# Prompt attention: where PE forms the former step's values in steps of at most four tiles

## The chip, the cores and the metric

The kernel runs on one core of one Trainium2 chip. The metric is the device time of one execution in microseconds, as the median of three runs.

## The reference

One layer of a hybrid decoder. RMSNorm and an adaLN modulation, one input projection for all heads, then attention for half of the channels and a short convolution for the other half, both gated by SiLU, an output projection, a gated residual, a last RMSNorm. There is a prompt of 1024 tokens and a sample part of 8 times 4 new tokens with a cache of 2048. The change touches the prompt's attention alone. It has 16 heads of 64 in two groups, and three branches: compressed blocks of 64 keys, selected blocks, and a window of 512. With 1024 keys there are 16 blocks and 16 are selected, so that the selected branch is plain causal attention.

```python
lg = jnp.einsum('bqghd,bngd->bghqn', qs, k_cmp) + tab[t5_bucket(d_cmp)].transpose(2, 3, 0, 1)
p_cmp = masked_softmax(lg, m_cmp)
o_cmp = jnp.einsum('bghqn,bngd->bqghd', p_cmp.astype(v_cmp.dtype), v_cmp)
...
lg = jnp.einsum('bqghd,bgqnkd->bghqnk', qs, ks) + b_sel.transpose(0, 1, 5, 2, 3, 4)
...
lg = jnp.einsum('bqghd,bwgd->bghqw', qs, k_win) + tab[t5_bucket(d_win)].transpose(2, 3, 0, 1)
...
return g[:, :, 0] * o_cmp + g[:, :, 1] * o_sel + g[:, :, 2] * o_win
```

## The kernel before

Each engine has its program written out by hand, and engines meet by semaphores. The prompt's attention is done in 32 units: a unit `u` is four heads on one tile of 128 queries. The tile is `TILE_ORDER[u % 8]` = 0, 2, 4, 6, 7, 5, 3, 1, so there are four passes of eight units. A unit has two steps, `w = 2u` for the selected branch and `w = 2u + 1` for window and compressed branch: 64 steps, 16 a pass. `tiles_of(w)` is the number of key tiles of a step: in a pass 1, 2, 3, 4, 5, 6, 7, 6, 8, 6, 6, 6, 4, 5, 2, 3. The last tile of an odd step is the compressed branch's.

A step has four quarters `h = 0..3`. PE's loop (L1456 to L1471) does in each: `scores(w + 2, h)`, the scores of head `h` two steps ahead (L1382, L1383, in one or two of four PSUM banks, and of the compressed branch L1388); in an odd step's first quarter the turning of the factors (L1414); the turns (transposes) of the tiles that `slots(w)` gives to the quarter (L1403, of the compressed branch L1400); and then, for turned tiles that are held, `values` (L1438, of the compressed branch L1429). Those that are left of the former step go in quarter 0.

```python
old = [x for x in held if x[0] < w]
go = len(old) if h == 0 else len(held) - 1 if h == 2 and len(held) >= 4 else 0
for x in held[:go]:
    values(*x)
```

A score waits (`score_prior`, `e_done`) until the exponential that last read its bank has ended: for one-bank scores that of four heads before, for two-bank scores (more than 512 keys) that of two heads before. A tile's values wait for its copy to SBUF.

The other engines follow the same steps and quarters. VectorE (the loop at L2454): `maxima(w + 2, h)` adds the position bias and takes the row minimum of the negated scores (L2392 or L2394 for far keys, L2395 for near ones); `factors(w + 1)` in quarter 0 (L2415); `first_factors` of an even step in quarter 1 (L2423, L2424, L2426 on the first query tile only, L2427); `selected_o` (L2435) in an odd step's quarter 1, which waits for the selected branch's values; `near_o(w // 2 - 1)` (L2441, L2443) in an even step's quarter 1, ahead of `maxima`, which waits for all values of the former unit. ScalarE copies turned tiles (L1916, L1914) and factors (L1906), and does the exponentials `exps(w + 2, h)` (L1893). POOL does `gate_o` behind `near_o`: an add (L1104) and a multiplication (L1108). SP stores the unit behind it.

Of the kernel before, what the change touches and what calls it, by code (L numbers as in the profile page):

```python
# [65 lines left out]
def build(nc: "bass.Bass", x_prompt, x_sample, cache_k_cmp, cache_v_cmp, cache_k_slc, cache_v_slc, cache_k_win,  # L66
# [27 lines left out]
    with ctx:  # L94
# [294 lines left out]
        def unit(u):  # L389
            return u // 8, TILE_ORDER[u % 8]  # L390

        def head_of(u, h):
            return 8 * (h // 2) + 2 * (u // 8) + h % 2
# [4 lines left out]
        def tiles_of(w):  # L398
            i = unit(w // 2)[1]
            return i + 1 if w % 2 == 0 else min(i + 1, 5) + 1  # L400

        def keys_of(w):

            k = (tiles_of(w) - w % 2) * P
            return k, {5: [384, 256], 6: [512, 256], 7: [384, 512], 8: [512, 512]}.get(k // P, [k])
# [11 lines left out]
        def cmp_bank(n):  # L417

            return score_bank[n] + (keys_of(n // 4)[0] > 384)

        def score_cols(b0, w):

            k, parts = keys_of(w)
            if len(parts) == 1:
                return PS[:, b0, 0:k]
            lo = 512 - parts[0] if len(parts) > 1 else 0
            return PS[:, b0:b0 + 2, :].rearrange("p a b -> p (a b)")[:, lo:lo + k]
# [5 lines left out]
        def slots(w):  # L433

            n = tiles_of(w)
            cuts = [(n * q + 2) // 4 for q in range(5)]
            return [range(cuts[q], cuts[q + 1]) for q in range(4)]
# [39 lines left out]
        class Chain:  # L477
# [4 lines left out]
            def link(self, ins):  # L482
                self.n += 1
                ins.then_inc(self.s, 1)
                self.eng.wait_ge(self.s, self.n)
# [686 lines left out]
        def _(pe):  # L1172
# [195 lines left out]
            def scores(w, h):  # L1368
                u, n, g = w // 2, 4 * w + h, h // 2
                i = unit(u)[1]  # L1370
                if h == 0:
                    pe.wait_ge(q_ld[u % 4], 16 * (u // 4 + 1))
                if score_prior[n] >= 0:
                    pe.wait_ge(e_done, score_prior[n] + 1)
                b0 = score_bank[n]
                q = qb[u % 4][:, h, :]
                kh, kl = (ksh, ksl) if w % 2 == 0 else (kwh, kwl)
                k, parts = keys_of(w)
                a = (i + 1) * P - k
                for c, m in enumerate(parts):  # L1380
                    x = 512 - m if c < len(parts) - 1 else 0
                    pe.matmul(PS[:, b0 + c, x:x + m], q, kh[:, g, a:a + m], start=True, stop=False)  # L1382
                    ins = pe.matmul(PS[:, b0 + c, x:x + m], q, kl[:, g, a:a + m], start=False, stop=True)  # L1383
                    a += m
                if w % 2 and h == 3:
                    for hh in range(4):
                        c0_ = 384 + 2 * NPB * hh
                        ins = pe.matmul(PS[:, cmp_bank(n), c0_:c0_ + 2 * NPB], qb[u % 4][:, hh, :], kcp[:, hh // 2, :], start=True, stop=True)  # L1388
                ins.then_inc(s_mm, 1)

            def turn_p(w, t):
                c = ring(w, t)
                if t == 0:
                    pe.wait_ge(e_done, 4 * w + 4)
                if w % 2 and t == tiles_of(w) - 1:
                    pe.wait_ge(c_pool, w // 2 + 1)
                if c >= 3:
                    pe.wait_ge(*turned(c - 3))
                if w % 2 and t == tiles_of(w) - 1:
                    pe.transpose(PS[:, turn_bank(c), 0:P], prc[w % 3][:, :, :].rearrange("p h n -> p (h n)"), ident[:, :]).then_inc(t_mm, 1)  # L1400
                    return
                for h in range(4):
                    ins = pe.transpose(PS[:, turn_bank(c), h * P:(h + 1) * P], pr[w % 3][:, h, t * P:(t + 1) * P], ident[:, :])  # L1403
                ins.then_inc(t_mm, 1)

            def turn_factors(u):

                c = ring0[2 * u + 1]
                pe.wait_ge(f_rdy, 2 * u + 2)
                if c >= 3:  # L1410
                    pe.wait_ge(*turned(c - 3))
                for a in range(2):
                    for j in range(2):
                        ins = pe.transpose(PS[:, turn_bank(c), P * (2 * a + j):P * (2 * a + j) + P], wide[:, a, j, :], ident[:, :])  # L1414
                ins.then_inc(t_mm, 1)
# [39 lines left out]
            held = []  # L1455
            for w in range(NI):  # L1456
                for h, part in enumerate(slots(w)):
                    if w + 2 < NI:
                        scores(w + 2, h)
                    if w % 2 and h == 0:  # L1460
                        turn_factors(w // 2)
                    for t in part:
                        turn_p(w, t)
                        held.append((w, t))
                    old = [x for x in held if x[0] < w]
                    go = len(old) if h == 0 else len(held) - 1 if h == 2 and len(held) >= 4 else 0
                    for x in held[:go]:
                        values(*x)
                    held = held[go:]
# [562 lines left out]
        def _(dve):  # L2032
# [344 lines left out]
            def maxima(w, h):  # L2377
                n, u = 4 * w + h, w // 2
                i = unit(u)[1]
                dve.wait_ge(s_mm, n + 1)  # L2380
                k, parts = keys_of(w)
                b0, r = score_bank[n], w % 3
                both = w % 2 and h == 3
                if both:
                    if u:
                        dve.wait_ge(ec_done, u)
                    dve.tensor_reduce(cs[:, :, :], PS[:, cmp_bank(n), 384:512].rearrange("p (h a n) -> p h n a", h=4, a=2), AX.X, ALU.add).then_inc(dch, 1)
                    chain.n += 1
                cols, low = score_cols(b0, w), nm[:, r, h:h + 1]
                far = max(0, k - 2 * P)  # L2390
                if far and w % 2 and i >= 4:
                    link(dve.tensor_tensor_reduce(cols[:, 0:far], cols[:, 0:far], edge[:, :], 1.0, 3.0e38, ALU.add, ALU.min, low))  # L2392
                elif far:
                    link(dve.tensor_reduce(low, cols[:, 0:far], AX.X, ALU.min))  # L2394
                dve.tensor_tensor_reduce(cols[:, far:k], cols[:, far:k], near[:, head_of(u, h), 2 * P - (k - far):2 * P], 1.0,  # L2395
                                         low if far else 3.0e38, ALU.add, ALU.min, low).then_inc(m_rdy, 1)
                if both:
                    dve.wait_ge(dch, chain.n)


                    m0, head = max(0, 2 * i - 2), head_of(u, 0)
                    cb = 2 * i + 2 - m0
                    row = tcmp[:, 2 * i - m0 + 1, head:head + 1]
                    tab = bass.AP(row.tensor, row.offset, [list(row.ap[0]), [8, NG], [1, 2], [-NH, cb]])
                    late = cs[:, :, m0:m0 + cb].rearrange("p (g j) n -> p g j n", g=NG)
                    link(dve.tensor_tensor(late, late, tab, ALU.subtract))
                    dve.tensor_reduce(nm[:, r, 4:8], cs[:, :, 0:2 * i + 2], AX.X, ALU.min).then_inc(c_rd, 1)
# [29 lines left out]
            def near_o(u):  # L2437
                dve.wait_ge(pv_mm, tile0[2 * u + 2])
                if u:
                    dve.wait_ge(mix_rdy, u)  # L2440
                link(dve.tensor_tensor(ow[:, :, :], PS[:, 6, 2 * P:4 * P].rearrange("p (j c) -> p j c", j=2), fac[:, 1, :, :], ALU.mult))  # L2441
                dve.wait_ge(sel_ev, u + 1)
                dve.tensor_tensor(mixs[u % 2][:, :, :], PS[:, 6, 0:2 * P].rearrange("p (j c) -> p j c", j=2), mixs[u % 2][:, :, :], ALU.add).then_inc(r_ev, 1)  # L2443
# [9 lines left out]
                        dve.tensor_copy(vcs[:, 4 * q:4 * q + 4, :], PS[0:NSB, 6 + q, :].rearrange("p (b c) -> p b c", c=DKV)).then_inc(c3_ev, 1)  # L2453
            for w in range(NI):  # L2454
                for h, part in enumerate(slots(w)):
                    if h == 1 and w % 2 == 0 and w:
                        near_o(w // 2 - 1)
                    if w + 2 < NI:
                        maxima(w + 2, h)
                    if w + 1 < NI and h == 0:  # L2460
                        factors(w + 1)
                    if w % 2 == 0 and h == 1:
                        first_factors(w // 2)
                    if w % 2 and h == 1:
                        selected_o(w // 2)
# [231 lines left out]
```

## Time and profile before

| | |
|---|---|
| median of three runs | 1491.7 us (1487.86 to 1492.43) |
| the profiled execution | 1485.97 us |
| its span | 1484.2 us |
| PE busy | 1421.5 us, 96% |
| VectorE busy | 960.4 us, 65% |
| ScalarE busy | 705.1 us, 48% |
| POOL busy | 236.9 us, 16% |
| PE's share of the chain that ended last | 88% |
| first step of the prompt's attention, last one's end | 745.4 us, 1206.7 us |

Busy time is the time in which an engine has an instruction under way, over the whole span. A share is a mean over stages: projections, compression, prompt attention, sample attention, output. The prompt attention is the stretch in the last line. Steps are told in the timeline by PE's factors (L1414), one group in each odd step, and by the keys of each score. In the second pass step 16 starts at 859.66 us, step 17 at 863.15, 18 at 868.64, 19 at 875.68, 20 at 883.32, 22 at 901.80 and 32 at 974.70; the third pass follows there.

### The profile page before, as it was taken

What the parts mean: (1) busy time and instruction counts of PE and PEld (TensorE: products, weight loads), DVE (VectorE), ACT (ScalarE), POOL (GpSimd) and SP (SyncE); (2) the same over time, 40 slices, a digit from 0 to 9 for tenths busy, and PEclk for the clock granted to TensorE, in tenths of its full rate; (3) what the DMA queues carried; (4) which work ended last, traced back from release to release, by engine and by line L of the source; (5) the groups of instructions that cost most, each with busy time, mean ns of one, the idle gap of its engine ahead of it and who ended that gap; (6) DMA issues with size and microseconds to landing.
All of it is one profiled execution on the core that took longest, in us unless ns stands there. A gap on an engine that the chain in (4) does not pass through costs nothing.

```text
span 1484.2 us, 27910 instructions
## 1 busy us (share of the span) xinstructions
PE 1421.5 (96%) x10526; PEld 1226.2 (83%) x10526; DVE 960.4 (65%) x2309; ACT 705.1 (48%) x1546; POOL 236.9 (16%) x447
## 2 busy tenths in 40 slices
PE   5999999999999999989989989989989999899998
PEld 1889999999999999977777777777777766688886
DVE  2646878878788787767676576576676563743226
ACT  2433233232322333266677777777777755621111
POOL 1101120110100101131021242232231141000000
PEclk9999999999999999999999999999999999999999
DMA  9335733332333423597221221221121049963321
GB/s 347 111 111 106 119 115 87 93 109 46 105 82 90 116 48 97 142 349 232 60 87 35 71 74 42 57 66 44 38 58 30 22 164 317 279 181 99 88 86 36
DMA packets 169862, 164.76 MB, mean 111 GB/s; under 512 B 53757, under 2 KB 150269, under 8 KB 164353
## 3 DMA queue, kind: packets, MB, share of 16 engines
q1 hardware_dynamic: 153904, 94.11, 23.1%
q0 software_dynamic: 15824, 68.87, 15.1%
q8 instruction: 84, 1.38, 0.4%
q14 instruction: 50, 0.40, 0.1%
HBM read 131.27 MB, written 35.83 MB: 113 GB/s over the span
## 4 chain that ended last, share of the span: by engine, by line
PE 88%; DVE 4%; DMA 3%; ACT 2%; issue 2%; SPq 1%; POOL 0%; DVEq 0%; ACTq 0%
PE PS L1266 33%; PE PS L1632 12%; PE PS L1438 8%; PE PS L1403 7%; PE PS L1382 5%; PE PS L1318 4%; PE PS L1383 4%; PE PS L1223 2%; PE PS L1224 2%; PE PS L1225 2%; DMA kwb<-in_cache_k_win 1%; DMA adaw<-in_ada_w 1%; PE PS L1485 1%; PE PS L1547 1%; PE PS L1414 1%
## 5 line engine op out<-in xcount | busy, mean ns | idle before, releaser
L1266 PEld LDWEIGHTS PS<-bo,wsl 128*128 128x128 f32 x4104 | 499.4, 188 | 0.4 <-issue 0.4
L1266 PE MATMUL PS<-bo,wsl 128*128 128x264 f32 x4104 | 499.6, 284 | 0.0
L1893 ACT ACTIVATE pr<-PS,nm 128x640 f32<-128x640 f32 (+7 forms) x256 | 181.3, 709 | 44.8 <-DVE nm L2395 42.2
L1728 ACT ACTIVATE wsl<-wsum 128x512 fp32r<-128x512 f32 x105 | 65.6, 631 | 237.8 <-DVE wsum L2118 237.8
L1916 ACT ACTIVATE ptt<-PS 128x512 f32<-128x512 f32 x264 | 149.8, 601 | 39.6 <-PE PS L1403 39.4
L1403 PE MATMUL PS<-ident,pr 128*128 128x128 f32 x1056 | 146.6, 273 | 0.3 <-ACT ptt L1916 0.3
L1438 PE MATMUL PS<-ptt,kvt 128*64 128x256 f32 x1056 | 136.2, 389 | 0.0
L1403 PEld LDWEIGHTS PS<-ident,pr 128*128 128x128 f32 x1056 | 122.1, 141 | 9.2 <-issue 0.6
L1438 PEld LDWEIGHTS PS<-ptt,kvt 128*64 128x64 f32 x1056 | 66.8, 136 | 41.1 <-issue 16.4
L2395 DVE CUSTOM_DVE_ANT_0 PS<-PS,near,nm 128x256 f32<-128x256 f32 x192 | 94.7, 493 | 6.8
L2394 DVE TENSOR_REDUCE nm<-PS 128x1 f32<-128x128 f32 (+5 forms) x128 | 70.5, 551 | 38.8 <-PE PS L1383 38.2
L2124 DVE TENSOR_TENSOR wsl<-wsum,wsl 128x512 fp32r<-128x512 f32 x105 | 70.9, 692 | 29.7 <-ACT wsl L1728 29.5
L1382 PE MATMUL PS<-ksh,qb 128*128 128x384 f32 (+3 forms) x192 | 75.9, 397 | 11.8 <-ACT pr L1893 10.5
L1632 PE MATMUL PS<-woh,mh 128*128 128x512 f32 x256 | 79.4, 391 | 0.0
L1632 PE MATMUL PS<-wol,mh 128*128 128x512 f32 x256 | 79.0, 390 | 0.0
L1632 PE MATMUL PS<-woh,ml 128*128 128x512 f32 x256 | 78.9, 389 | 0.0
L2570 DVE TENSOR_TENSOR ml<-mr,mh 128x1024 fp32r<-128x1024 f32 x16 | 19.6, 1226 | 90.7 <-ACT mh L1989 90.6
L1382 PE MATMUL PS<-kwh,qb 128*128 128x384 f32 (+3 forms) x192 | 70.8, 370 | 6.9 <-ACT pr L1893 6.9
L1318 PE MATMUL PS<-xt,w 128*128 128x273 f32 x256 | 72.1, 404 | 4.9 <-DVE xt L2347 2.6
L2118 DVE TENSOR_TENSOR wsum<-wr 128x512 f32<-128x512 f32 x105 | 68.5, 685 | 1.2 <-DMA wr<-in_w_in 1.2
L2347 DVE COPY xt<-PS 64x256 f32<-64x256 f32 x128 | 54.0, 422 | 23.3 <-PE PS L1312 19.5
L1989 ACT ACTIVATE mh<-mr 128x1024 fp32r<-128x1024 f32 x16 | 17.0, 1061 | 100.7 <-PE PS L1632 100.0
(358 smaller groups left out, 2422.0 us busy)
## 6 DMA issues: line engine op xcount, KB each, us to landing
wr<-in_w_in SPq DMA_DIRECT2D x32, 512.0 KB, 5.6
adaw<-in_ada_w SPq DMA_DIRECT2D x8, 1024.0 KB, 9.4
wr<-in_w_in SPq DMA_DIRECT2D x32, 256.0 KB, 4.5
q_stacked<-qp POOLq DMA_DIRECT2D x64, 128.0 KB
qb<-q_stacked SPq DMA_DIRECT2D x32, 256.0 KB, 3.0
mr<-mixed SPq DMA_DIRECT2D x16, 512.0 KB, 3.8
mixed<-yy POOLq DMA_DIRECT2D x16, 264.0 KB
xb<-in_x_prompt POOLq DMA_DIRECT2D x8, 512.0 KB, 4.5
```

Of the source, the lines that this page charges most:

```text
L1266: ins = pe.matmul(PS[:, 2 * q + c, 0:H // 2], w[:, x, kk, :], b[:, y, kk, c * H // 2:(c + 1) * H // 2], start=(first and kk == 0 and x == ...
L1318: ins = pe.matmul(PS[:, 4 + g, 0:CB], w1[c][:, m, :], xt[m // 4 % 2][:, m % 4, g, :], start=(m == 0), stop=(m == 31))
L1382: pe.matmul(PS[:, b0 + c, x:x + m], q, kh[:, g, a:a + m], start=True, stop=False)
L1403: ins = pe.transpose(PS[:, turn_bank(c), h * P:(h + 1) * P], pr[w % 3][:, h, t * P:(t + 1) * P], ident[:, :])
L1438: ins = pe.matmul(PS[64 * g:64 * g + 64, 6, a:a + 2 * P], v, pt[tc % NPT5][:, 2 * g:2 * g + 2, :].rearrange("p j c -> p (j c)"), start=(t ...
L1632: ins = pe.matmul(PS[0:n, b0 + c, :], a[:, k, 0:n], b[k][:, 512 * c:512 * c + 512], start=(k == 0 and a is mh and b is woh), stop=(k == 15 ...
L1893: act.activation(pr[r][:, h, 0:k], score_cols(b0, w), ACT.Exp, scale=-1.0, bias=nm[:, r, h:h + 1], accum_out=rsum[:, r, h:h + 1]).then_inc ...
L1916: act.activation(pt[tc % NPT5][:, :, :], PS[:, turn_bank(c), :].rearrange("p (h c) -> p h c", h=4), ACT.Copy).then_inc(pt_act, 1)
L2118: dve.tensor_tensor(wsum[(sums_to(m) - 1) % 2][:, :, :], raw(*a), raw(*b), op).then_inc(w_sum, 1)
L2124: dve.tensor_tensor(wsl[m % NSLOT][:, 1, :, :], source(m), f32(wsl[m % NSLOT][:, 0, :, :]), ALU.subtract).then_inc(w_lo, 1)
L2394: link(dve.tensor_reduce(low, cols[:, 0:far], AX.X, ALU.min))
L2395: dve.tensor_tensor_reduce(cols[:, far:k], cols[:, far:k], near[:, head_of(u, h), 2 * P - (k - far):2 * P], 1.0, low if far else 3.0e38, A ...
```

## The change

In steps of at most four tiles (`few`), PE forms the values that are left of the former step in the second quarter, behind that quarter's scores and turns, and not in the first. On VectorE `near_o`, which waits for those values, goes behind the second quarter's `maxima` in these steps. In other steps both stay.

```diff
-                    go = len(old) if h == 0 else len(held) - 1 if h == 2 and len(held) >= 4 else 0
+                    few = tiles_of(w) <= 4
+                    go = len(old) if h == (1 if few else 0) else len(held) - 1 if h == 2 and len(held) >= 4 else 0
...
                 for h, part in enumerate(slots(w)):
-                    if h == 1 and w % 2 == 0 and w:
+                    few = tiles_of(w) <= 4
+                    if h == 1 and w % 2 == 0 and w and not few:
                         near_o(w // 2 - 1)
                     if w + 2 < NI:
                         maxima(w + 2, h)
+                    if h == 1 and w % 2 == 0 and w and few:
+                        near_o(w // 2 - 1)
```

In the changed kernel VectorE's lines have numbers higher by one. ScalarE and POOL keep their order.

PE in step 18 (three tiles), from the first quarter's turn to the second's; a two-bank score is L1382 and L1383 twice each. Before:

```order
L1403 MATMUL PS<-ident,pr 128x128 x4
L1438 MATMUL PS<-ptt,kvt 64x256 x2
L1429 MATMUL PS<-ptt,vcp 64x128 x4
L1382 MATMUL PS<-ksh,qb 128x384
L1383 MATMUL PS<-ksl,qb 128x384
L1382 MATMUL PS<-ksh,qb 128x256
L1383 MATMUL PS<-ksl,qb 128x256
L1403 MATMUL PS<-ident,pr 128x128 x4
```

The same piece in the changed kernel:

```order
L1403 MATMUL PS<-ident,pr 128x128 x4
L1382 MATMUL PS<-ksh,qb 128x384
L1383 MATMUL PS<-ksl,qb 128x384
L1382 MATMUL PS<-ksh,qb 128x256
L1383 MATMUL PS<-ksl,qb 128x256
L1403 MATMUL PS<-ident,pr 128x128 x4
L1438 MATMUL PS<-ptt,kvt 64x256 x2
L1429 MATMUL PS<-ptt,vcp 64x128 x4
```

The values (L1438, L1429) have moved behind the second score and the second turn.

VectorE in the second quarter of step 18 before, with `near_o` (ow, mixs), the maximum (nm) and the first branch's factors (rsum, rrec, rg):

```order
L2415 RECIPROCAL rrec<-rsum 128x4
L2441 TENSOR_TENSOR ow<-PS,fac 128x256
L2443 TENSOR_TENSOR mixs<-PS,mixs 128x256
L2394 TENSOR_REDUCE nm<-PS 128x1
L2395 ISA PS,nm<-PS,near,nm 128x256
L2395 ISA nm 128x1
L2423 TENSOR_REDUCE rsum<-prc 128x4
L2424 RECIPROCAL rrec<-rsum 128x4
L2427 TENSOR_TENSOR rg<-rrec,sg 128x4
```

The same piece in the changed kernel:

```order
L2416 RECIPROCAL rrec<-rsum 128x4
L2395 TENSOR_REDUCE nm<-PS 128x1
L2396 ISA PS,nm<-PS,near,nm 128x256
L2396 ISA nm 128x1
L2442 TENSOR_TENSOR ow<-PS,fac 128x256
L2444 TENSOR_TENSOR mixs<-PS,mixs 128x256
L2424 TENSOR_REDUCE rsum<-prc 128x4
L2425 RECIPROCAL rrec<-rsum 128x4
L2428 TENSOR_TENSOR rg<-rrec,sg 128x4
```

`near_o` has moved from ahead of the maximum to behind it, and stands right ahead of the factors.

## Rows read from the trace of the kernel before

**Rows 1.** The page's first part: busy time, share of the span and instructions

```profile
PE 1421.5 (96%) x10526; PEld 1226.2 (83%) x10526; DVE 960.4 (65%) x2309; ACT 705.1 (48%) x1546; POOL 236.9 (16%) x447
```

**Rows 2.** Windows, steps 16, 17, 18, 19, 22 to 31: from:to length, then each engine's busy time

```profile
859.66:863.15 3.49, 3.49 (x31) 2.74 (x30) 2.76 (x13) 2.34 (x11) 1.79 (x4) 1.00 0.54 159
863.15:868.64 5.49, 4.30 (x27) 3.08 (x26) 5.19 (x25) 4.49 (x15) 2.37 (x6) 1.00 0.34 96
868.64:875.68 7.04, 5.39 (x40) 4.49 (x40) 6.29 (x22) 5.26 (x15) 3.57 (x7) 1.00 0.27 76
875.68:883.32 7.64, 6.78 (x49) 5.54 (x49) 4.22 (x17) 5.94 (x14) 0.70 (x2) 1.00 0.13 36
...
901.80:974.70 72.90, 72.90 (x579) 57.05 (x579) 45.14 (x169) 56.19 (x140) 21.38 (x45) 1.00 0.18 51
```

The engines are in the order PE, weight loads, VectorE, ScalarE, POOL; then granted clock, DMA share and GB/s.

**Rows 3.** Waits of PE over the stage: us in total, times, longest

```profile
PE PS L1382 <- ACT pr L1893: 17.4, 23, 1.8
```

**Rows 4.** Timeline of PE, steps 18, 19: start, us, engine, line, tiles, count, [idle before]

```profile
869.87 0.65 PE L1438 MATMUL PS<-ptt,kvt 128*64 128x256 f32 x4
...
870.89 0.45 PE L1382 MATMUL PS<-ksh,qb 128*128 128x384 f32 x1
...
877.34 1.52 PE L1438 MATMUL PS<-ptt,kvt 128*64 128x256 f32 x12
878.79 0.44 PE L1382 MATMUL PS<-kwh,qb 128*128 128x384 f32 x1
...
879.84 0.42 PE L1382 MATMUL PS<-kwh,qb 128*128 128x384 f32 x1
...
881.87 0.44 PE L1382 MATMUL PS<-kwh,qb 128*128 128x384 f32 x1 [0.76 <-ACT pr L1893]
```

**Rows 5.** Timeline of ScalarE, steps 18 and 19

```profile
869.91 0.19 ACT L1893 ACTIVATION_READ_ACCUMULATOR pr<-PS,nm 128x1 f32 x1
...
874.68 0.79 ACT L1893 ACTIVATE pr<-PS,nm 128x640 f32<-128x640 f32 x1 [0.82 <-DVE nm L2395]
...
880.12 0.60 ACT L1916 ACTIVATE ptt<-PS 128x512 f32<-128x512 f32 x1 [1.25 <-PE PS L1403]
```

**Rows 6.** Timeline of VectorE, steps 18 and 19

```profile
871.00 0.42 DVE L2441 TENSOR_TENSOR ow<-PS,fac 128x256 f32<-128x256 f32 x1 [0.28 <-PE PS L1429]
...
871.80 0.55 DVE L2394 TENSOR_REDUCE nm<-PS 128x1 f32<-128x384 f32 x1
872.39 0.49 DVE L2395 CUSTOM_DVE_ANT_0 PS<-PS,near,nm 128x256 f32<-128x256 f32 x1
...
873.22 0.37 DVE L2427 TENSOR_TENSOR rg<-rrec,sg 128x4 f32<-128x4 f32 x1
873.52 0.55 DVE L2394 TENSOR_REDUCE nm<-PS 128x1 f32<-128x384 f32 x1
...
879.68 0.57 DVE L2392 CUSTOM_DVE_ANT_0 PS<-PS,edge 128x384 f32<-128x384 f32 x1 [1.87 <-PE PS L1383]
...
881.09 0.56 DVE L2392 CUSTOM_DVE_ANT_0 PS<-PS,edge 128x384 f32<-128x384 f32 x1
```

**Rows 7.** Timeline of PE, the first turn of step 13

```profile
846.25 0.63 PE L1403 MATMUL PS<-ident,pr 128*128 128x128 f32 x4 [0.26 <-ACT ptt L1916]
```

**Rows 8.** Timeline of POOL, step 18

```profile
871.97 0.74 POOL L1104 TENSOR_TENSOR mixs<-mixs,ow 128x256 f32<-128x256 f32 x1 [0.35 <-DVE mixs L2443]
872.85 0.72 POOL L1108 TENSOR_TENSOR mixs<-mixs,zau 128x256 f32<-128x256 f32 x1
```

**Rows 9.** Timelines: L2426 in steps 16 and 32, POOL in step 32

```profile
863.78 0.23 DVE L2426 TENSOR_SCALAR rrec<-rrec,anyc 128x4 f32<-128x4 f32 x1
...
978.83 0.66 DVE L2426 TENSOR_SCALAR rrec<-rrec,anyc 128x4 f32<-128x4 f32 x1
...
978.73 0.73 POOL L1108 TENSOR_TENSOR mixs<-mixs,zau 128x256 f32<-128x256 f32 x1
```

**Rows 10.** Timeline of VectorE, step 63: selected_o

```profile
1203.40 0.42 DVE L2435 TENSOR_TENSOR mixs<-PS,fac 128x256 f32<-128x256 f32 x1 [1.04 <-PE PS L1438]
```

## The prediction

> **What bounds the kernel now.** The page comes first: TensorE is busy for nearly all of the span [rows 1]. But that is a share over stages with different limits, so the next view was the windows of the prompt attention, cut at the steps of its second pass through the tile order (steps 16 to 31) [rows 2]. The reader is to see two kinds of steps. From step 22 to 31 PE is busy for all of 72.90 us, although steps 28, 30 and 31 are among the short ones that the change reorders: nothing is to be had there by moving PE's work. PE's idle time stands in step 17 (5.49 - 4.30 = 1.2 us), step 18 (7.04 - 5.39 = 1.65) and step 19 (7.64 - 6.78 = 0.86): 3.7 us a pass. The waits over the stage say who ends it: PE waited 17.4 us for ScalarE's exponentials, in 23 waits [rows 3]; the longest, 1.8, lies before the first step, so 15.6 us lie in the four passes. That is the ceiling of any gain here, 1% of the time.
>
> Then the timelines, to find what ScalarE waits for when PE waits for it. In step 19 PE forms three tiles of values from 877.34 to 878.79 and only then the second scores. VectorE has stood idle 1.87 us when they come (879.68), ScalarE 1.25 (880.12), and PE then waits at 881.87, 0.76 us [rows 4 to 6]: a circle through three engines with the values standing in it. Step 18 looks alike, but VectorE is busy there for 6.29 of 7.04 us, and in step 17 for 5.19 of 5.49 [rows 2]. So step 19 is held by late scores, steps 17 and 18 mostly by VectorE.
>
> **What the change does, part by part.** No instruction is added, removed or resized, no DMA moves, and POOL and ACT keep their order. On PE the values go behind the second quarter's scores and turns in steps 0 to 3, 12, 14 and 15 of each pass (the first step of all has no former values, and step 62 no scores to go behind). On VectorE near_o goes behind that quarter's maxima, because the values that it needs are now later.
>
> *Steps 28, 30, 31 and their like.* The values move past one score and at most a turn; PE has no gap, and the third quarter's scores start when they did. Price 0; the cover is PE's own full queue, and without it they would cost what step 18 costs, below. In the first pass alone PE waits 0.26 us at the first turn of step 13 for a ScalarE copy [rows 7]. The change frees a maximum, and with it that copy, early; I take the whole wait back: **-0.25 us, once**.
>
> *Step 19 by itself.* The second score starts 1.45 us sooner, at 877.34 for 878.79. Score and turns take 879.84 - 878.79 = 1.05, then the values run, and the third score starts at 877.34 + 1.05 + 1.45 = 879.84, as before [rows 4]. A score is out 0.89 us after its start (878.79, VectorE at 879.68), so the third is out at 880.73, and VectorE took it at 881.09 only because the second had made it late [rows 6]. Gain **0.35 to 0.4 us** at the start of step 20, which PE's queue keeps through the full steps. ScalarE's 1.25 us vanish, but only 0.4 of them stood in the circle: next late is the third score itself, on PE.
>
> *Step 18.* The second score can't start where the values start now (869.87), because its bank is free only when ScalarE has read out the exponential before: 869.91 + 0.19 = 870.10 [rows 4, 5]. So it starts at 870.15, 0.74 early; score and turns take 1.05, the values 1.02 (870.89 - 869.87), and they end at 872.2 for 870.9: 1.3 us late. VectorE does the maximum first (1.08 us from 871.80, shifted by 0.74 to 871.06), then near_o, which took 0.8 us (871.00 to 871.80) and now starts at 872.3: 873.1 [rows 6]. Behind near_o stand the first branch's small factors and the third maximum, on which ScalarE's next exponential hangs directly (874.68, after 0.82 us idle) [rows 5]. POOL stands behind near_o too: its add started at 871.97, released by near_o's second product, and took 0.74 [rows 8]. Shifted by the same 1.3, it runs from 873.25 to 874.0, over the small product L2427, due at 873.5. What does that cost? The same product took 0.37 us from 873.22 and ended at 873.59, with POOL's multiplication (872.85 + 0.72) [rows 6, 8]; and L2426, as small, took 0.23 us in the second pass and 0.66 in the third, where POOL multiplied from 978.73 for 0.73 [rows 9]. I read both as waiting for POOL. Then the third maximum starts at 873.97 for 873.52: 0.45 us late. If nothing waited for POOL it would be 0.13; these are the ends, and I take 0.45 because both rows end with POOL's. So step 18 loses what step 19 wins, and leaves **+0.05 us a pass, +0.2 in four**.
>
> The Trainium skill says in SBUF — State Buffer, "Who interferes with whom", that a VectorE instruction with two SBUF inputs contends with a GpSimd one that reads SBUF, and that the later one "fully blocks". By that rule the sum is the one with 0.45; if both ran freely it would be about 1.3 us lower over four passes. The trace agrees with it, by 0.66 against 0.23 us.
>
> *Step 16* has the same order on both engines, with a one-bank score ahead of the values, so less than 1.05 us. Here near_o is late by less, and the factors behind it meet POOL's add as in step 18. Bounds 0 and step 18's 0.45; I take 0.25, the middle. In the third and fourth pass L2426 stands behind POOL already, which cost 0.66 - 0.23 = 0.43 [rows 9] and needn't come twice: 0.25 - 0.43 = -0.2. VectorE is full through step 17, so this is passed on. In the first pass step 0 has nothing to move. Together 0.25 - 0.4 = **-0.15**. Step 17 moves one tile; its early score gains nothing at a full VectorE.
>
> *The end of the stage.* The last selected_o starts at 1203.40, after VectorE had idled 1.04 us for the values of step 62 [rows 10]. Now the turns of step 63's second quarter lie ahead, at most 0.63 us [rows 7]. The last values wait for selected_o, but also for a ScalarE copy that comes sooner. Between 0 and 0.63 I take **+0.2**.
>
> Sum: -0.25 + 0.2 - 0.15 + 0.2 = 0.0 us. The profiled execution took 1485.97 us and would stay there; the median of the three shown is 1491.7 (1487.86 to 1492.43), and a sum of zero leaves it there. What a measurement of this kernel can tell from no change is about 0.3%, 4.5 us.
>
> **The rivals.** *Forecast*: idle time changes its place, 1491.7; its own range is 1488 to 1495 (0.5 us a pass up or down, alike in all passes, makes 2 us; the rest is the spread of the times shown).
> *A small gain.* Nothing waits for POOL: step 18 costs 0.13, step 16 hardly anything, and each pass keeps 0.3 to 0.5 us: 1489.9. Against it [rows 9]; for it, that these are few and short rows.
> *A true gain.* The circle opens: steps 18 and 19 give back nearly all of PE's idle time, 1.65 + 0.86, so 2.4 us a pass, 9.6 in all: 1482.1. It needs near_o to come in VectorE's idle time at step 18; for it speak the 0.8 us that VectorE has free there, against it that the values come late just by that.
> *Slower.* VectorE stands in near_o and selected_o for values that PE now gives last, and this isn't won back: 0.45 in step 18, 0.25 in step 16, 0.2 in step 14, and in step 19 selected_o takes the 0.4 back: 1.3 us a pass, 5.2 in all, 1496.9. It decides from 1.1 us a pass on, where it is told from no change. Against it: the third score of step 19 needs 0.89 us itself after the values, which covers selected_o, and PE's full queue covers step 14.
> *The change does nothing*: it shows in the rows of both engines, so only by cancelling, which is the forecast.
>
> **How the numbers follow.** Forecast 0.62, small gain 0.18, true gain 0.13, slower 0.07. So faster by over 0.3%: 0.13; within: 0.80; slower: 0.07. The range, 1486.5 to 1495.5, holds the first two with their spread and the nearer edges of the others.
>
> **What would show it.** In the profile of the changed kernel: VectorE's idle 1.87 us in step 19 gone, and PE's wait late in that step gone or under 0.2; PE's idle time in step 18 up from 1.65 to about 2.1; step 18's small product near 0.5 us with POOL's add over it; step 18 longer by 0.45 us, step 19 shorter by 0.4; steps 22 to 31 at 72.9. It is wrong if step 18 doesn't grow, or if steps 16 to 19 together move by over 1 us.

## The result, and the profile after

The changed kernel took 1497.48 us in the median of seven runs (1494.07 to 1501.34), the kernel before 1489.12 in seven (1486.76 to 1492.43): a ratio of 1.005, with an interval from 1.0033 to 1.0068. It is slower, by more than the 0.3% that a measurement can tell. A later comparison of the same two kernels gave 1.0021 (0.999 to 1.0052), which alone can't be told from no change; so the size is uncertain, between about 3 and 8 us. The forecast was no change.

The execution of the changed kernel that was profiled is its slowest, 1501.34 us, with a span of 1499.6. Its page's first part, as [rows 1]:

```profile
PE 1429.1 (95%) x10526; PEld 1236.4 (82%) x10526; DVE 964.3 (64%) x2309; ACT 703.7 (47%) x1546; POOL 236.8 (16%) x447
```

PE is busy 7.6 us longer with the same number of instructions: the same work ran slower. Of this, 4.4 us lie in the prompt attention (443.94 for 439.56 us, the two stage windows below), the rest behind it. The windows of steps 16, 17, 18, 19 and 22 to 31, cut as in [rows 2] (from:to, length, busy PE, weight loads, VectorE, ScalarE, POOL; then the granted clock, the share of full speed that TensorE's clock was given), say where:

```profile
859.23:862.77 3.54, 3.54 (x31) 2.77 (x30) 2.73 (x14) 3.04 (x14) 1.85 (x4) 1.00 0.60 175
862.77:868.62 5.85, 4.19 (x27) 3.06 (x27) 5.56 (x24) 3.62 (x13) 2.33 (x6) 1.00 0.32 90
868.62:877.44 8.82, 6.75 (x40) 5.70 (x41) 6.73 (x23) 5.14 (x15) 3.53 (x7) 0.81 0.16 42
877.44:884.71 7.27, 6.52 (x49) 5.51 (x50) 4.81 (x18) 5.90 (x14) 0.70 (x2) 1.00 0.23 61
903.20:976.06 72.86, 72.86 (x580) 57.11 (x580) 45.43 (x169) 56.08 (x140) 21.50 (x45) 1.00 0.18 51
```

Step 19 is 0.37 us shorter and steps 22 to 31 are what they were. Step 18 is 1.78 us longer, and in its row stands what none of [rows 2] has: a granted clock of 0.81. PE's idle time over the four steps, length less busy time, is 4.5 us (0 + 1.66 + 2.07 + 0.75) where [rows 2] have 3.7. The timeline of PE there, to set beside [rows 4]:

```profile
868.65 0.42 PE L1382 MATMUL PS<-ksh,qb 128*128 128x384 f32 x1 [1.22 <-ACT pr L1894]
...
869.34 1.05 PE L1403 MATMUL PS<-ident,pr 128*128 128x128 f32 x4
870.13 0.69 PE L1382 MATMUL PS<-ksh,qb 128*128 128x384 f32 x1
...
871.36 1.05 PE L1403 MATMUL PS<-ident,pr 128*128 128x128 f32 x4
872.35 0.80 PE L1438 MATMUL PS<-ptt,kvt 128*64 128x256 f32 x4
...
874.80 0.60 PE L1403 MATMUL PS<-ident,pr 128*128 128x128 f32 x4
...
877.47 0.42 PE L1382 MATMUL PS<-kwh,qb 128*128 128x384 f32 x1 [2.08 <-ACT pr L1894]
```

Four transposes take 1.05 us from 869.34 and from 871.36, and 0.60 at 874.80. Score and turns, 870.13 to 872.35, take 2.2 us where [rows 4] have 1.05. The windows of these stretches alone:

```profile
869.27:872.69 3.42, 3.42 (x16) 2.91 (x16) 2.47 (x11) 2.40 (x7) 1.88 (x4) 0.50 0.32 81
985.33:988.74 3.41, 3.28 (x13) 3.31 (x14) 2.18 (x10) 2.37 (x7) 1.83 (x4) 0.50 0.28 76
995.57:998.98 3.41, 3.41 (x17) 2.70 (x17) 1.84 (x9) 2.86 (x6) 0.70 (x2) 0.50 0.14 41
1111.62:1115.03 3.41, 3.41 (x16) 3.41 (x15) 1.21 (x5) 2.17 (x6) 0.70 (x2) 0.50 0.40 116
```

Half the clock, 1.2 of 2.4 GHz, in steps 18, 34, 35 and 51. Ahead of the first, PE had idled 0.46 us at 865.72 and 1.22 at 868.65; ahead of the one in step 35, 1.93 us. The kernel before, in the same part of its second pass, idled 1.22, 1.14 and 0.51 us, and its clock stayed at 1.00. From PE's first score of the loop to the start of step 63 the stage takes 461.9 us for 455.9 (a step starts where the weights of its first score are loaded):

```profile
745.32:1207.25 461.93, 443.94 (x3367) 350.18 (x3368) 301.75 (x1103) 345.64 (x858) 119.14 (x252) 0.98 0.18 49
```

The same row of the kernel before:

```profile
745.37:1201.24 455.87, 439.56 (x3367) 344.47 (x3367) 297.82 (x1103) 346.80 (x858) 119.27 (x252) 1.00 0.18 50
```

VectorE and POOL in step 18, as [rows 6] and [rows 8]: near_o late, POOL's add right behind it, and the small product of the factors (L2428) under that add for 0.50 us.

```profile
873.63 0.42 DVE L2442 TENSOR_TENSOR ow<-PS,fac 128x256 f32<-128x256 f32 x1 [0.89 <-PE PS L1429]
...
874.85 0.50 DVE L2428 TENSOR_TENSOR rg<-rrec,sg 128x4 f32<-128x4 f32 x1
875.27 0.55 DVE L2395 TENSOR_REDUCE nm<-PS 128x1 f32<-128x384 f32 x1
```

```profile
874.60 0.74 POOL L1104 TENSOR_TENSOR mixs<-mixs,ow 128x256 f32<-128x256 f32 x1 [3.00 <-DVE mixs L2444]
```

The profiled span is 15.4 us over before's, of which 6.1 are in this stage and 9.4 behind it. Those 9.4 don't come with the change: when the changed kernel was run again (below), its stage was as long (462.0) and its rest 282.4, before's being 282.9.

### The profile page after: what moved, and what is told of

Read it like the earlier page. It is cut to its first block, busy times and chain, and to the rows that moved or that the text cites. A ratio compares the mean times of both kernels' runs of the same rounds, so it can differ in the third digit from the quotient of the medians.

```text
span 1499.6 us, 27910 instructions
## 1 busy us (share of the span) xinstructions
PE 1429.1 (95%) x10526; PEld 1236.4 (82%) x10526; DVE 964.3 (64%) x2309; ACT 703.7 (47%) x1546; POOL 236.8 (16%) x447
## 4 chain that ended last, share of the span: by engine, by line
PE 87%; DVE 4%; DMA 4%; ACT 2%; issue 2%; SPq 1%; POOL 0%; DVEq 0%; ACTq 0%
PE PS L1266 33%; PE PS L1633 12%; PE PS L1438 8%; PE PS L1403 7%; PE PS L1382 5%; PE PS L1318 4%; PE PS L1383 4%; DMA kwb<-in_cache_k_win 2%; PE PS L1223 2%; PE PS L1224 2%; PE PS L1225 2%; PE PS L1429 1%; DMA wkr<-in_w_in 1%; PE PS L1590 1%; PE PS L1414 1%
## 5 line engine op out<-in xcount | busy, mean ns | idle before, releaser
L1438 PE MATMUL PS<-ptt,kvt 128*64 128x256 f32 x1056 | 136.7, 390 | 0.4 <-ACT ptt L1915 0.4
L1438 PEld LDWEIGHTS PS<-ptt,kvt 128*64 128x64 f32 x1056 | 67.3, 137 | 41.4 <-issue 16.8
L1382 PE MATMUL PS<-ksh,qb 128*128 128x384 f32 (+3 forms) x192 | 77.2, 403 | 10.5 <-ACT pr L1894 9.4
L1382 PE MATMUL PS<-kwh,qb 128*128 128x384 f32 (+3 forms) x192 | 71.6, 374 | 10.3 <-ACT pr L1894 10.3
L1383 PE MATMUL PS<-ksl,qb 128*128 128x384 f32 (+3 forms) x192 | 65.7, 350 | 0.0
```

Source lines behind the costliest of these rows:

```text
L1438: ins = pe.matmul(PS[64 * g:64 * g + 64, 6, a:a + 2 * P], v, pt[tc % NPT5][:, 2 * g:2 * g + 2, :].rearrange("p j c -> p (j c)"), start=(t ...
```

## The experiments

Two theories. *A*: PE's idle stretches, drawn together by the reorder, bring the granted clock down, and PE's work behind them runs at half speed. *B*: near_o comes late on VectorE, and the circle through ScalarE and PE with it; the clock is a bystander.

The measure is the stage, from the first score of PE's loop to the start of step 63. It repeats: 461.93 and 462.05 us in two profiles of the changed kernel, step by step within 0.15. Whole times spread by several us, and the stage shows only a part of that. The stage is read from one profiled execution of each kernel; the times are of several executions, each beside runs of the kernel before on the same chip. *Half clock* is the number of stretches with a granted clock of 0.5 within the steps. Steps 18 and 19 are those of the second pass. The last column is the granted clock over the whole span, averaged over the executions that the times are taken from.

| kernel | step 18 | step 19 | half clock | stage | time against before | clock |
|---|---|---|---|---|---|---|
| before | 7.04 | 7.64 | 1 (at the start) | 455.9 | 1 | 0.987 (70) |
| changed | 8.82 | 7.27 | 4, and the start | 461.9 | 1.005 (1.0033 to 1.0068) | 0.984 (7) |
| changed, again | 8.93 | 7.27 | 4, and the start | 462.0 | 1.0021 (0.999 to 1.0052) | 0.984 (10) |
| changed, fillers | 7.67 | 7.28 | 0 | 456.5 | 0.9989 (0.9965 to 1.0013) | 0.989 (10) |
| odd steps alone | 7.03 | 7.27 | 1 | 455.6 | 0.9982 (0.9962 to 1.0003) | 0.988 (10) |
| even steps alone | 8.77 | 9.23 | 5, and the start | 465.0 | 1.0029 (1.0012 to 1.0046) | 0.984 (9) |
| before, fillers | 7.04 | 7.64 | 1 (at the start) | 456.1 | 0.9973 (0.9953 to 0.9993) | 0.990 (12) |
| odd steps, fillers | 7.04 | 7.28 | 0 | 454.3 | 0.9979 (0.9952 to 1.0007) | 0.989 (12) |
| PE's half, fillers | 9.99 | 7.59 | 4, and the start | 471.5 | 1.0076 (1.0053 to 1.0099) | 0.985 (6) |
| VectorE's half, fillers | 7.94 | 7.65 | 1 (at the start) | 460.9 | one execution, 1490.72 us | 0.991 (1) |
| factors first, fillers | 6.88 | 7.27 | 1 (at the start) | 452.7 | 0.9946 (0.9926 to 0.9966) | 0.990 (7) |
| factors first | 6.88 | 7.27 | 1, and the start | 452.6 | 0.9982 (0.9951 to 1.0013) | 0.986 (12) |
| fillers elsewhere | 7.67 | 8.85 | 3 | 469.0 | one execution, 1498.99 us | 0.986 (1) |
| fillers before step 3 only | 7.67 | 7.27 | 2, and the start | 460.3 | one execution, 1491.35 us | 0.988 (1) |

The number of executions stands behind each clock. The median of before beside the three single ones is 1490.11 us. The last column tells whether the profiled executions are typical. The changed kernel has the lower clock on average too, 0.9841 for 0.9873, and with the fillers the clock is back. But the profiled execution of before, at 0.991, is above its average, and its 1485.97 us are below its medians. So the 6.1 us may be more than the change costs in the stage on average. My estimate: in the profiles, four stretches, 13.7 us at half clock, cost 5.4 us; an average clock lower by 0.0032 over 1490 us means 9.5 us at half clock (2 x 0.0032 x 1490), which at the same rate cost 3.8 us. It is for the whole span, since an execution that wasn't profiled doesn't tell where its clock fell.

**The changed kernel again.** No edit.

> The changed kernel once more, as a control. The prompt attention, from PE's first score of the loop to the start of step 63, took 455.9 us before and 461.9 with the change. Theory A (the granted TensorE clock falls to half behind PE's lengthened idle stretches at steps 17 to 19, which then run slow): again some stretches at 0.5 in the first half of a pass, each making step 18 or 19 longer by 1.0 to 1.6 us over 7.7 and 7.3, and the stage 459 to 463 by how many there are. Theory B (near_o's lateness alone, the clock no matter): the stage is 461.9 again whatever the clock shows.

The same steps fell to half clock as in the first profile of the changed kernel (18, 34, 35, 51), with nearly the same lengths, and the stage was 462.05. That the pattern repeats speaks for a cause in the order of work; it doesn't yet choose between the theories.

**Fillers in PE's idle time.** Transposes of the identity that nobody reads, into the bank of the next turn, ahead of waiting scores:

```diff
+                    if h == 0 and w % 16 in (2, 3):
+                        pe.wait_ge(*turned(ring0[w] - 3))
+                        for _ in range(8):
+                            pe.transpose(PS[:, turn_bank(ring0[w]), 0:P], ident[:, :], ident[:, :])
                     if w + 2 < NI:
                         scores(w + 2, h)
```

The later kernels take the number of fillers from a table, `{(step in the pass, quarter): number}`; for this one it would be `{(2, 0): 8, (3, 0): 8}`.

> The changed kernel, and PE does eight transposes of the identity (about 0.9 us, into the bank of the next turn) ahead of the first scores of steps 2 and 3 of each pass, where it idles for 1.3 and 2.2 us; nothing waits for them. Theory A: the stretches at half clock in steps 18, 19 and their like go, step 18 is 7.5 to 7.7 and step 19 7.3 us in every pass, the stage 456 to 457.5 and the time 4 to 6 us under the changed kernel. Theory B: the clock's stretches may go, but the stage stays at 460 or more, since near_o is as late as before.

The windows of step 18, of step 19 and of the stage in this kernel:

```profile
867.83:875.50 7.67, 6.44 (x48) 5.39 (x49) 6.67 (x23) 5.14 (x15) 3.52 (x7) 1.00 0.18 47
875.50:882.78 7.28, 6.52 (x49) 5.52 (x50) 4.82 (x18) 5.91 (x14) 0.70 (x2) 1.00 0.22 61
...
744.55:1201.04 456.49, 444.51 (x3431) 349.84 (x3431) 301.47 (x1103) 345.04 (x858) 118.92 (x252) 1.00 0.18 50
```

The clock is 1.00 through the stage, and the stage 5.4 us shorter, though PE does 64 transposes more and none of the reorder was undone. That is theory A, and the stage is under the 460 that theory B put as the least. What is left, 456.5 against 455.9, is the reorder's own price in the stage at full clock: +0.6.

**Fillers elsewhere**, the control: the same number ahead of steps 8 and 9 (`{(8, 0): 8, (9, 0): 8}`).

> A control for the fillers: the changed kernel with the same 16 transposes a pass ahead of the first scores of steps 8 and 9, where PE has no idle time. Theory A: they cost their own time there, 0.9 us each and 7 in all, and the stretches at half clock in steps 18, 19, 34, 35, 51 and their like stay as in the changed kernel: the stage 467 to 470. If fillers acted otherwise than by filling idle time, some of the four would go.

```profile
747.01:1216.03 469.02, 449.70 (x3432) 354.52 (x3432) 302.54 (x1103) 346.10 (x858) 118.75 (x252) 0.99 0.18 49
```

They cost their time (0.88 us each) and half clock stayed, though in other steps: 2, 19 and 34, the last of its stretches double as long (the step took 9.96 us for 7.67). The places were not those of the changed kernel, 18, 34, 35 and 51. That part of the expectation missed: with the same order of work and the passes shifted against each other by some us, other steps were hit. This is one execution, and since hits move, a hit that is missing from one place proves little; what the run shows is that fillers away from the idle time don't keep the clock.

**Fillers ahead of step 3 alone** (`{(3, 0): 8}`).

> The changed kernel with eight transposes ahead of step 3's first scores alone (the longest idle stretch, 2.2 us), none ahead of step 2's (1.3). It tells which idle time the clock's fall hangs on. Theory A with the long stretch alone: no half clock, the stage 456.5. If the 1.3 us ahead of step 2, with the 0.6 in step 1, do it: the stretches in step 18 and 34 stay, those in steps 35 and 51 go, the stage 458.5 to 459.

The stage was 460.3. Step 3 and its like were never hit, 7.27 us in all passes; step 2 of the third and fourth pass was (9.26 and 8.78 us for 7.67). So the 1.2 us ahead of step 2, together with the wait in step 1, are enough by themselves. That the long idle stretch accounts for the hits in step 3 fits, but one execution doesn't prove it. The size came out 1.5 us over the expected; the first pass began with a longer stretch at half clock here, and its steps 0 and 2 took 3.26 and 8.21 us for 2.36 and 7.67.

**Before, with fillers** (`{(2, 0): 8, (2, 3): 8, (3, 0): 4, (3, 3): 4}`, in the kernel before).

> The kernel before, with transposes of the identity in PE's idle time of steps 2 and 3 of each pass (8 ahead of the first and last scores of step 2, 4 ahead of those of step 3; 0.9 and 0.45 us). Theory A (the clock is what the fillers act on): before had no stretch at half clock in the passes beyond the one at their very start, so there is nothing to win: the stage stays at 455.5 to 456.5 us. Rival (fillers help in some other way, for instance by what a PE after an idle stretch does): step 18 and 19 get shorter than 7.04 and 7.64, the stage 454 or less.

456.1, with steps 18 and 19 as before: fillers do nothing to a step whose clock is whole. The time, however, was 0.9973 of before's, with an interval that leaves out 1, for a kernel whose stage is no shorter. The last column has a likely cause: its executions were granted 0.990 on average, those of before beside it 0.987; the difference, 0.0028, is worth 3.3 us at the rate of the estimate above. Before's 24 go from 1484.77 us at 0.992 to 1498.69 us at 0.981. So the kernel before too loses clock in executions that weren't profiled, and fillers seem to give some of it back; in which steps isn't shown.

**Odd and even steps alone**, and odd steps with fillers:

```diff
-                    few = tiles_of(w) <= 4
+                    few = tiles_of(w) <= 4 and w % 2 == 1
```

and `w % 2 == 0` for the other, on PE and VectorE alike.

> The change in odd steps alone (1, 3, 15 of each pass); even ones as before, near_o too. Theory A: step 19 is 7.3 us in place of 7.64 wherever the clock holds, step 18 stays at 7.04, so the stage is 454 to 455, 1 to 2 us under before, unless a stretch at half clock falls in. Theory B: the same 454 to 455, since near_o is untouched. If reordering values as such were bad, it would be over 456.

> The change in even steps alone (0, 2, 12, 14 of each pass), with near_o behind the maxima there. Theory A: step 18 is 7.5 to 7.7 us, or 8.7 where the clock halves, step 19 7.6, or 9 with half clock; the stage 458 to 463. Theory B: step 18 longer by a fixed 0.5 to 0.6, the stage 458 to 459 and no pass differs from another.

> The change in odd steps alone, with the fillers. Theory A: no stretch at half clock in the passes, step 18 at 7.03 and step 19 at 7.27 in all four, the stage 454.1 to 454.4 us, 1.6 us under before, and the time about as much under it (0.1%, at the edge of what a measurement tells). Rival: the stretch at half clock in step 34 has another source and comes again, 455.5.

The fillers of the last are `{(2, 0): 8, (2, 3): 8, (3, 0): 4}`. Odd alone, step 19 is 7.27 us in every pass, 0.37 won each time, and near_o isn't touched. One half clock fell in at step 34 (8.41 us for 7.03) and took the most of it back; with fillers it is gone, and the stage is 454.3, the 1.6 us under before that were expected. Even alone is the harm: step 18 at 8.77 us with half clock, and 465.0 for the stage, 2 us over what I had expected, since it has step 18's loss, none of step 19's gain, and five hits.

**One half of the change at a time**, with fillers: `few = False` on VectorE (PE's half alone, fillers `{(2, 0): 8, (3, 0): 8}`), or on PE (VectorE's half alone, `{(2, 0): 8, (2, 3): 8, (3, 0): 4, (3, 3): 4}`).

> PE's half of the change alone, with the fillers: near_o stays ahead of the second quarter's maximum and makes VectorE wait for the late values there. Theory B in its part (PE's half is what makes near_o late, VectorE's half softens it): values end at 872.3 in step 18's time, near_o 873.1, only then the maximum 874.2 and factors, so step 18 is 8 to 8.6 us for 7.67, and the stage 458 to 460. Rival (VectorE's half is the harm, its order brings the product under POOL's add): step 18 under 7.67, the stage under 456.5.

> VectorE's half of the change alone, with fillers: values stay in the first quarter on PE, near_o goes behind the maximum of the second. Theory B: in step 18 the maximum waits for scores that still come behind the values (871.75), near_o follows at 872.9, POOL's add stands over the small product again, and the third maximum starts near 874.4 for 873.5: step 18 is 7.8 to 8.1 us for 7.04, step 19 7.64, the stage 459 to 461. Rival (near_o's place is no matter by itself): 456.

With PE's half alone near_o stops VectorE ahead of the maximum:

```profile
874.39 0.17 DVE L2422 RECIPROCAL rrec<-rsum 128x4 f32<-128x4 f32 x1
876.35 0.42 DVE L2448 TENSOR_TENSOR ow<-PS,fac 128x256 f32<-128x256 f32 x1 [1.78 <-PE PS L1429]
876.80 0.42 DVE L2450 TENSOR_TENSOR mixs<-PS,mixs 128x256 f32<-128x256 f32 x1
877.15 0.55 DVE L2401 TENSOR_REDUCE nm<-PS 128x1 f32<-128x384 f32 x1
```

Step 18 was 9.99 us, over the expected 8 to 8.6, and the stage 471.5: PE stood idle for 2.17 us in one wait of step 18, ahead of its last score, where no fillers are, and the clock halved behind this wait in step 2 of all four passes. VectorE's half alone gave 7.94 and 460.9, as expected. Each half by itself is worse than both together with fillers (456.5). VectorE's half is needed for PE's, and neither wins.

**The factors ahead of near_o.** In short steps, with and without fillers:

```diff
-                    if h == 1 and w % 2 == 0 and w and few:
-                        near_o(w // 2 - 1)
                     if w + 1 < NI and h == 0:
                         factors(w + 1)
                     if w % 2 == 0 and h == 1:
                         first_factors(w // 2)
+                    if h == 1 and w % 2 == 0 and w and few:
+                        near_o(w // 2 - 1)
```

> The changed kernel with fillers, and in short steps the first branch's factors go ahead of near_o. POOL's add, which near_o releases, then can't stand over their small product. If the product's wait for POOL is worth what the trace says (0.50 us in place of 0.17), the product is at 0.17 to 0.2 us, step 18 is 7.3 to 7.4 us for 7.67, step 16 or 17 up to 0.3 less too, and the stage 454.5 to 455.5 for 456.5. If it was no wait for POOL, the product stays long and the stage at 456.5.

> ff_first_warm without its fillers: the change, with the first branch's factors ahead of near_o. Its idle time before step 19 is shorter than the changed kernel's by 0.7 to 0.8 us. Theory A says that the clock falls where PE's idle time is long and close together, so fewer stretches at half clock than the changed kernel's four: none to two, the stage 452.7 plus 1.0 to 1.6 us for each, 452.7 to 456. If the fillers matter little here, 452.7 and the time of ff_first_warm, 0.5% under before.

VectorE in step 18 of the kernel with fillers:

```profile
873.72 0.17 DVE L2430 TENSOR_REDUCE rsum<-prc 128x4 f32<-128x24 f32 x1
873.92 0.18 DVE L2431 RECIPROCAL rrec<-rsum 128x4 f32<-128x4 f32 x1
874.14 0.16 DVE L2434 TENSOR_TENSOR rg<-rrec,sg 128x4 f32<-128x4 f32 x1
874.22 0.43 DVE L2448 TENSOR_TENSOR ow<-PS,fac 128x256 f32<-128x256 f32 x1
```

```profile
870.31:877.19 6.88, 6.43 (x48) 5.39 (x49) 6.21 (x23) 5.14 (x15) 3.52 (x7) 1.00 0.24 63
...
747.00:1199.70 452.70, 446.00 (x3431) 352.66 (x3432) 297.29 (x1103) 344.88 (x858) 118.64 (x252) 0.99 0.17 48
```

The product takes 0.16 us for 0.50, and its group now fits into the time in which near_o had to wait for values anyway. Both help, and the run doesn't part them. Step 18 is 6.88, 0.8 under the changed kernel with fillers and 0.16 under before; the expected 7.3 was too little. The stage is 3.2 us under before, and the time 1483.33 us for before's 1490.87 (0.9946, 0.9926 to 0.9966): a version that beats both. The stage explains under half of those 7.5 us. The average clock, 0.9896 for 0.9871, is worth about 3 us more at the rate of the estimate above, and wherever in the span that was won. Without fillers the stage is the same, 452.6, with one hit at step 34 (7.97 us), and the time 0.9982 (0.9951 to 1.0013), which can't be told from before.

## Why the prediction was wrong

The step that failed is the sum's silent assumption that PE's idle time costs only itself. "Forecast: idle time changes its place" priced a place at zero. But PE's work behind an idle stretch ran at half clock, 1.0 to 1.6 us more for each of four steps, 5.4 us in all (461.9 against 456.5 with fillers; about 3.8 on average by the estimate above). No term and no rival held it: the slower rival gave 1496.9, near the measured 1497.48, by another mechanism: VectorE standing in selected_o and giving step 19's gain back. VectorE did wait there, 0.68 us at 881.69, and step 19 was still 0.37 us shorter. The row was there to read. Each line of [rows 2] carries the granted clock. It was 1.00 in all of them, and I never asked what would keep it there, nor named it as a thing to watch. Even the kernel before has one stretch at half clock in this stage, at its start, from 746.73 us, behind PE's longest wait (1.82 us).

Point by point, at full clock (from the kernel with fillers, unless said):

- *Step 19 by itself*, gain 0.35 to 0.4: the size is right, 7.64 to 7.28, the reading half. VectorE's 1.87 us idle are 0.22 in the changed kernel. But PE's wait late in the step, 0.76 us at 881.87, hasn't gone: it has moved to the first score of step 20, the row below. PE's idle time in the step fell by 0.11 us alone (0.86 to 0.75), and 0.26 of the gain is PE's busy time (6.78 to 6.52), which the prediction had as unchanged.
- *Step 18*, loss 0.45: too small, 0.63. The order of events went as told: the score 1.5 us after the step's start, values last, the product under POOL's add, 0.50 us long. The missing 0.17 is in PE's turns: followed by values they take 0.53 us (870.03 to 870.56 in that kernel's timeline), followed by a score 0.36. I had taken score and turns as 1.05 in either order. In step 19 this cancels, since the turns before and after the move exchange their followers.
- *Step 16 and what is passed on*: +0.25, then -0.2. Measured over steps 16 and 17, 8.98 to 9.38 us in the second pass (+0.4) and 9.42 to 9.38 in the third (-0.04). Sign right in both, the gain smaller; and a -0.2 in the first pass that I had left out. The gain is smaller because the small factor (in the changed kernel L2427), 0.66 us behind POOL before, is still 0.52 behind POOL's add.
- *First pass, step 13*: -0.25, measured -0.34 (7.79 to 7.45).
- *Steps 22 to 31*: 72.86 for 72.90, price 0. Right.
- *End of the stage*: +0.2; near_o's second product began 4.98 us after step 63's start before (1206.22 from 1201.24) and 5.18 after (1212.43 from 1207.25). Right.
- *What would show it*: "PE's idle time in step 18 up from 1.65 to about 2.1": 8.82 - 6.75 = 2.07. "PE's wait late in that step gone or under 0.2": no, 0.75. "It is wrong if steps 16 to 19 together move by over 1 us": they moved from 23.66 to 25.48 us, 1.8. It was wrong by its own test, and by the clock.
- *"A small gain. Nothing waits for POOL"*: refuted, both by 0.50 us and by the kernel with the factors first, where the product is at 0.16. The 0.66 against 0.23 us that the prediction set beside the skill's rule are of a `tensor_scalar`, with one tensor and a column of constants; the instruction with two SBUF tensors, which the rule is about, is the product.

The row of PE's wait at the first score of step 20:

```profile
884.74 0.42 PE L1382 MATMUL PS<-ksh,qb 128*128 128x384 f32 x1 [0.75 <-ACT pr L1894]
```

So the reorder costs +0.6 us in the stage and +0.2 behind it at full clock, where I had 0.0 in all. That is a miss of under a microsecond, and the rest of what the stage lost is the clock. The medians are 8.4 us apart in the first comparison and 2.7 in the second, so the 2.3 us that the first has over the stage's 6.1 have no cause shown.

## What to carry to other kernels

A reorder that costs next to nothing at full clock, and adds 0.8 us to 3.7 us of idle time, can still draw TensorE's idle stretches together (one of 2.08 us for 1.14 and 0.51), and the work behind them then ran at half speed for a while. Where a stage has such stretches, look at the granted clock by window before and after, and cost a hit at the work that follows; and compare the profiled execution's clock with that of the other executions, before its stage is taken as typical. A measure inside the trace, such as the length of the stage, tells 0.5 us in a kernel whose whole time scatters by 5. And when a wait is moved, put the independent work of the waiting engine into it: the factors ahead of near_o were worth more than the change itself.

## What the runs showed that I had not expected

With hardly a difference in PE's rows between passes, one pass was hit and another not: in the changed kernel step 18 took 8.82 us in the second pass and 7.67 in the first and fourth, and the same steps were hit in a second profile (8.93). With fillers in steps 8 and 9 other passes were hit. And a hit needs no more idle time than the kernel before has. In the kernel with the factors first and no fillers, step 34 was hit with 1.22 us idle ahead of it, as long as before's wait at the same place, which was at full clock:

```profile
982.58 0.42 PE L1382 MATMUL PS<-ksh,qb 128*128 128x384 f32 x1 [1.22 <-ACT pr L1894]
```

So something besides the length of the idle time decides. That it is its place in time is my reading; what the chip goes by in detail wasn't tried and stays open.

Eight transposes ahead of a wait, 1.0 us of PE's time, kept the clock whole where 2.0 us of idle time had halved it, even with 1.0 us of idle time left (the kernel with fillers, ahead of step 19):

```profile
875.53 0.42 PE L1382 MATMUL PS<-kwh,qb 128*128 128x384 f32 x1 [1.02 <-ACT pr L1898]
```

The Trainium skill speaks in SBUF — State Buffer, "Who interferes with whom", of VectorE and GpSimd blocking each other by who comes first. The trace bears it out twice more: the product is 0.50 us long when it comes behind POOL's add, and 0.16 when it comes ahead. It holds over the whole changed kernel: of its 32 products, 16 took over 0.4 us, and each of these ended within 0.03 us of a POOL instruction that had begun first; the other 16 took 0.16 or 0.17.
